# Second attention of a two-block transformer step: three weight splits cut into quarter pieces

## The chip, the cores and the metric

One core of a Trainium2 chip runs the whole program in one launch. The metric is the device time in microseconds (us); the median of several executions counts. Of an execution with the profiler on there is a trace, with the begin and end of each engine's instructions.

TensorE (PE in the rows) multiplies, ScalarE (ACT) and VectorE (DVE) work element by element, GpSimd (POOL) computes a few inverse roots, and SyncE (SP) issues nearly all loads.

## The reference, cut to what matters

256 tokens of width 1024, float32, batch 1. The first block is a modulated transformer layer: `h = rms_norm(x) * (1 + sc) + sh`, one projection `h @ w_in`, two attentions, gates, a projection `w_out` and a gated feed-forward part. The second block has four feed-forward parts, a short convolution and a compressed/selected/window attention. The change lies in the first block only:

```python
proj = h @ w_in[l]
(q_a, k_a, v_a, q_i, k_i, w_i, q_b, k_b, v_b, gate_a, gate_b) = jnp.split(proj, split_at, axis=-1)
o_a = dsa_attention(q_a, k_a, v_a, q_i, k_i, w_i)   # 4 heads of 128; each query keeps the 64 keys
                                                    # of highest index score
o_b = moba_attention(q_b, k_b, v_b)                 # 4 heads; with 256 tokens plain causal attention
merged = sigmoid(gate_a) * (o_a @ w_br_dsa[l]) + sigmoid(gate_b) * (o_b @ w_br_moba[l])
x = x + gt_m * (merged @ w_out[l])
```

## The kernel before, in words

**Products.** Float32 accuracy comes from three products of rounded halves: every operand is held as a high part (`fp32r`) and a low part, and `three` (L1713 to L1717) issues high times high, weight-low times high, weight-high times low. A weight unit is 128x2048 words (1 MB), four row blocks of 512 columns. A product of 1024 rows by 512 columns takes two units, each 24 matmuls of 512 columns.

**A unit's way.** SyncE loads it into one of three raw slots (`raw_ring`, L771). ScalarE rounds it into `w_hi_ring` (`split`, L910 to L917) when the raw slot is full and TensorE has used the unit three earlier. VectorE subtracts it into `w_lo_ring` (`lo_split`, L1244 to L1247), and by that tells TensorE that the unit is ready and SyncE that the raw slot is free (`raw_done`). SyncE goes through its list of loads in order, each waiting for the load three earlier to be freed. Modulation rows (`mod`, `mod_row`, `mod_sum`) use the same raw slots; TensorE reads them raw (L1853).

**The order of work** is one list, written by hand in `make_plan`. Each engine goes through the whole list and issues what is its own, so the list is the order of each engine's queue. `part(stage, chunk, number, parts, after, inside, held)` adds a unit: its matmuls, in four quarters where `inside` has four lists, with `inside[q]` behind quarter q; then the items of `after`; and then, unless `held`, `then split`, which splits all units up to the third one further.

**The units here**: V0 and V1 (`va`), then G0 to G3 (`gb`: chunk 0 parts 0 and 1, chunk 1 parts 0 and 1), B0, A0, B1, A1 (`bb`, `ba`) and `out1`. Before the change G1 is split behind V0, G2 behind V1, G3 behind G0, B0 behind G1, A0 behind G2.

**The second attention** (`dsa`) has eight items (four heads, two tiles of 128 queries) laid between the quarters of G0, G1 and G2 by `attention` and `spread`. Step i holds: `qk` i on TensorE (L1967, 128 wide for even items, 256 for odd ones); `sm` i on VectorE (L1547: mask, scale, maximum) and the exponential on ScalarE (L1128); transpose of the probabilities of item i-1 on TensorE (L1936), copied by ScalarE for even items (L1046) and by VectorE for odd ones (L1405); `pv` i-2 on TensorE (L1974), scaled by VectorE (L1551, L1554). The ten steps are spread over twelve quarters: G0 has none behind its first, then steps 0, 1, 2; G1 has 3, 4, none, 5; G2 has 6, 7, 8, 9. Behind G2 stand the transposes of `o` (L1882), which wait for the last scaled output.

**Top-k** (L1525 to L1537, VectorE) masks all but 64 keys of a query tile by rounds of `max` and `match_replace`, in four pieces per tile; the last one also writes `mask_d`, which the `sm` of this attention read.

Of the kernel before, what the change touches and what calls it, by code (L numbers as in the profile page):

```python
# [7 lines left out]
ALU = mybir.AluOpType  # L8
ACT = mybir.ActivationFunctionType
F32 = mybir.dt.float32  # L10
# [13 lines left out]
RING = 3  # L24
# [66 lines left out]
def make_plan():  # L91


    plan, units = [], []
# [14 lines left out]
    def tgroup(stage, n, **a):  # L109
        return [dict(a, kind="tp", stage=stage, g=g) for g in range(n)]  # L110
# [112 lines left out]
        if not last:  # L223
            add("then split", unit=u)

    def part(stage, chunk, number, parts, after=(), inside=(), held=False):


        subs = len(inside) if inside else 1
        for q in range(subs):  # L230
            add("lin", stage=stage, chunk=chunk, part=number, parts=parts, unit=len(units), sub=q, subs=subs)
            if inside:
                plan.extend(inside[q])
        units.append((stage, chunk, number))
        for a in after:
            plan.extend(a)
        if not held:
            add("then split", unit=len(units) - 1)
# [4 lines left out]
    def evac(stage, chunk=0):  # L243
        return [dict(kind="evac", stage=stage, chunk=chunk)]
# [4 lines left out]
    def mod(m, half):  # L249
        return [dict(kind="mod", m=m, half=half)]  # L250
# [4 lines left out]
    def mod_row(m, half):  # L255
        return [dict(kind="tp", stage="mrow", g=m, c=half)]
# [4 lines left out]
    def mod_sum(m):  # L261
        return [dict(kind="tp", stage="mod", g=m)]

    def topk(tt, piece):
        return [dict(kind="topk", tt=tt, piece=piece)]
# [34 lines left out]
    part("qa", 0, 1, 2, [mod_row(7, 1), evac("qa"), mod(8, 0)])  # L300
    part("ka", 0, 0, 2, [mod_sum(7), mod_row(8, 0), mod(8, 1), topk(1, 1)])
    part("ka", 0, 1, 2, [tgroup("qa", 2), mod_row(8, 1), evac("ka"), mod(9, 0)])
    part("va", 0, 0, 2, [mod_sum(8), mod_row(9, 0), mod(9, 1), topk(1, 2)])
    part("va", 0, 1, 2, [tgroup("ka", 2), mod_row(9, 1), evac("va"), topk(1, 3)])
    steps = attention([dict(b="dsa", h=h, tt=tt) for h in range(NH) for tt in range(TT)])
    inside = spread(steps, 3)
    part("gb", 0, 0, 2, [], inside[0])
    part("gb", 0, 1, 2, [evac("gb")], inside[1])
    part("gb", 1, 0, 2, [tgroup("o", 4)[:2]], inside[2])
    part("gb", 1, 1, 2, [evac("gb", 1), tgroup("o", 4)[2:]])  # L310
    add("sigmoid")
    part("bb", 0, 0, 1, [mod(10, 0)])
# [66 lines left out]
    for item in plan:  # L379
        if item["kind"] == "then split":  # L380
            split(item["unit"] + RING)
            continue
        full.append(item)
        if item["kind"] == "lin" and "sub" not in item:
            split(item["unit"] + RING)
        if item["kind"] == "gp":
            split(item["unit"] + RING)
        if item["kind"] == "ffn":
            n = 3 * NJ
            item["have"] = s  # L390
            s = min(item["unit"] + n + RING, len(units))
# [21 lines left out]
    for item in full:  # L413
        k = item["kind"]
        item["n"] = number("kind " + k)
        if k == "split":
            unit_raw[item["unit"]] = transfer("unit", item["unit"])
        if k == "mod":
            item["raw"] = transfer("mod", item["m"], item["half"])
        if k == "lin" and item["part"] == 0 and item.get("sub", 0) == 0:  # L420
            if (item["stage"], item["chunk"]) in (("cm", 0), ("qg", 0), ("wo", 0)) and count["pi"] % 2:
                number("pi")
            pi = THIRD if (item["stage"], item["chunk"]) == ("qg", 1) else number("pi")
            pi_of[item["stage"], item["chunk"]] = item["pi"] = pi
            item["pair_before"] = count.get(f"pair{pair_no(pi)}", 0)
        elif k in ("lin", "evac"):
            item["pi"] = pi_of[item["stage"], item["chunk"]]
        if k == "lin" and item.get("by_tt") and item["sub"] == 0:
            item["half"] = number("half")
        if k == "evac":  # L430
            st = item["stage"]
            if item.get("tt") == 0:
                item["half"] = count["half"] - 1
            if st not in ("out1", "co", "wo") and item.get("tt") != 0:
                pair_after[item["pi"]] = number(f"pair{pair_no(item['pi'])}") + 1
            if st in ("qi", "qb", "kb", "qa", "ka"):
                item["rope"] = number("rope")
            if st in ("qb", "kb", "qa", "ka", "qg") or (st == "kv" and item["chunk"]):
                item["nq"] = number("nq")
        if k == "cmp" and item["s"] == 0:  # L440
            item["nq"] = number("nq")
        if k == "tp":
            item["tg"] = number("tg")
            if item["stage"] == "mrow":
                item["of"] = number("mrow") // 2
            if item["stage"] in PAIRED:
                item["hl"] = number("hl")
            if item["stage"] != "p" and last_p is not None and item["tg"] - last_p[0] <= 2:
                item["outputs"] = last_p[1] + 1
            if item["stage"] == "p":  # L450
                last_p = item["tg"], count.get("it tp", 0)
        if k == "ffn":
            item["tg"], item["hl"], item["gi"] = number("tg", NJ), number("hl", NJ), number("gi", NJ)
            for u in range(item["have"], min(item["unit"] + 3 * NJ + RING, len(units))):
                unit_raw[u] = transfer("unit", u)
        if k == "xh":
            item["hl"] = number("hl")
        if k == "gp" and item["half"]:
            item["gi"] = number("gi")
        if k == "gt":  # L460
            item["tg"], item["gi"] = number("tg"), count["gi"] - 1
        if k in ("gu", "ffn", "nsa"):
            item["pairs_before"] = [count.get(f"pair{q}", 0) for q in range(2)]
        if k in ("qk", "sm", "pv") or (k == "tp" and item["stage"] == "p"):
            item["it"] = number("it " + k)
# [33 lines left out]
def turn(r):  # L499

    return (r - EARLY) // RING + 1
# [6 lines left out]
def two_block_program(nc, A, out):  # L508
# [40 lines left out]
    with ExitStack() as ctx:  # L549
# [5 lines left out]
        def sem(name):  # L555
            if name not in sems:
                sems[name] = ctx.enter_context(nc.semaphore(name))
            return sems[name]
# [339 lines left out]
        def _(act):  # L898
# [11 lines left out]
            def split(u, r, gate):  # L910

                act.wait_ge(sem(f"raw_full{r % RING}"), 32 * turn(r))
                if gate is not None:

                    act.wait_ge(sem("unit_used"), gate)
                words = unit_size(u)
                act.activation(w_hi[:, u % RING, 0:words], raw[:, r % RING, 0:words], ACT.Copy)\  # L917
                   .then_inc(sem("hi_ready"), 1)

            for item in plan:  # L920
# [5 lines left out]
                if k == "split":  # L926
                    u = item["unit"]
                    split(u, unit_raw[u], u - RING + 1 if u >= RING else None)
                if k == "square":
                    n = item["n"]  # L930
                    if n == 0:
                        act.wait_ge(sem("x_full"), 16)
                    else:
                        act.wait_ge(sem("x_ready"), 4 * xu[n])
                        act.wait_ge(sem("rstd_ready"), n)
                    if n == 6:
                        act.wait_ge(sem("qss_ready"), find["nq", "kv", 2] + 1)
                    for tt in range(TT):
                        ins = act.activation(junk[:, :], x[:, tt, :], ACT.Square, accum_out=ss[:, tt:tt + 1])
                        tick.step(ins) if tt < TT - 1 else ins.then_inc(sem("ss_ready"), 1)  # L940
# [298 lines left out]
        def _(dve):  # L1239
# [4 lines left out]
            def lo_split(u, r, two=lambda a: 0):  # L1244
                dve.wait_ge(sem("hi_ready"), u + 1 + two(3))
                words = unit_size(u)
                dve.tensor_tensor(w_lo[:, u % RING, 0:words], raw[:, r % RING, 0:words],  # L1247
                                  w_hi[:, u % RING, 0:words].bitcast(F32), ALU.subtract).then_inc(sem("raw_done"), 1)
# [74 lines left out]
            for item in plan:  # L1323
# [3 lines left out]
                    lo_split(u, unit_raw[u])  # L1327
                if k == "split":
                    lo_split(item["unit"], unit_raw[item["unit"]])
                if k == "init":  # L1330
                    dve.wait_ge(sem("init_done"), 1)
                    tick(dve.tensor_copy(cols1[:, :], bank[4][:, 0:P]))
                    dve.tensor_copy(cols2[:, :], bank[4][:, P:P + 56]).then_inc(sem("cols_ready"), 1)
                    dve.wait_ge(sem("cols_ready"), 1)
# [795 lines left out]
```

## Time and profile before

| | us |
|---|---|
| median of 3 runs | 1532.31 (1532.15 to 1532.56) |
| the profiled execution | 1530.0 |
| its span | 1528.0 |
| TensorE busy | 1465.4 (96%) |
| VectorE busy | 850.2 (56%) |
| ScalarE busy | 688.6 (45%) |
| GpSimd busy | 37.4 (2%) |
| second attention, first matmul of G0 to the transposes of `o` | 191.98 to 225.41 |

Durations of matmuls overlap, since the next one begins while the last drains: the time from one start to the next is what TensorE spends on one. Times of day in the text are us from the start of the span. The granted clock is that of TensorE, 1.00 for 2.4 GHz and 0.50 for 1.2 GHz.

### The profile page before, as it was taken

The numbers are of one execution on the slowest core, as the hardware profiler recorded it, in microseconds if no ns is written. First come the engines' busy times: TensorE is split into PE (matmuls) and PEld (weight loads), VectorE is DVE, ScalarE is ACT, GpSimd is POOL, SyncE is SP. The second block draws the span as 40 slices with busy tenths as digits, with TensorE's granted clock in tenths as the row PEclk, the third lists the DMA queues.
The fourth block names the chain that finished last, engine by engine and source line by source line (L and its number), as shares of the span: only waits on it lengthen the run. The fifth ranks groups of instructions, "written<-read, shape, count | busy, mean of one in ns | idle before, by whom it ended". The sixth has DMA issues, their size and how long they took to land.

```text
span 1528.0 us, 18024 instructions
## 1 busy us (share of the span) xinstructions
PE 1465.4 (96%) x6944; PEld 1169.2 (77%) x6944; DVE 850.2 (56%) x1023; ACT 688.6 (45%) x866; POOL 37.4 (2%) x53
## 2 busy tenths in 40 slices
PE   6989979999999999999999999989999988999998
PEld 3647667688888888888888888778888765788887
DVE  2676756554545554456764445566445567654453
ACT  2535444353334444444454444744444575554432
POOL 0010100000000000000000000210000020000000
PEclk9999999999999999999999999999999998999999
DMA  9853845555555566546555555555655430255552
GB/s 338 280 187 111 269 145 189 169 180 184 188 191 162 197 193 192 191 140 220 173 185 193 179 181 190 145 165 193 193 190 176 163 110 1 86 190 184 180 191 78
DMA packets 187881, 270.11 MB, mean 177 GB/s; under 512 B 8351, under 2 KB 134119, under 8 KB 187817
## 3 DMA queue, kind: packets, MB, share of 16 engines
q1 hardware_dynamic: 186448, 267.01, 53.5%
q10 hardware_dynamic: 1208, 1.94, 0.4%
q0 software_dynamic: 160, 0.26, 0.2%
q8 instruction: 44, 0.72, 0.2%
q14 instruction: 21, 0.16, 0.0%
HBM read 268.15 MB, written 1.05 MB: 176 GB/s over the span
## 4 chain that ended last, share of the span: by engine, by line
PE 84%; DVE 6%; ACT 4%; DMA 3%; issue 2%; POOL 0%; SPq 0%; ACTq 0%; DVEq 0%
PE bank L1715 25%; PE bank L1717 25%; PE bank L1716 25%; DVE w_lo_ring L1247 2%; ACT w_hi_ring L917 2%; PE bank L1745 2%; DMA raw_ring<-in_w_in_dram 1%; PE bank L1853 1%; PE bank L1882 1%; PE bank L2037 1%; PE bank L1940 1%; DMA raw_ring<-in_w_out_dram 1%; DMA arena<-in_w_mod_dram 1%; PE bank L2016 0%; DVE h_lo L1380 0%
## 5 line engine op out<-in xcount | busy, mean ns | idle before, releaser
L1247 DVE TENSOR_TENSOR w_lo_ring<-raw_ring,w_hi_ring 128x2048 fp32r<-128x2048 f32 x231 | 525.2, 2277 | 427.9 <-ACT w_hi_ring L1199 332.4
L1715 PE MATMUL bank<-w_hi_ring,h_hi 128*128 128x512 f32 x1360 | 544.1, 400 | 8.2 <-DVE h_lo L1380 3.1
L1717 PE MATMUL bank<-w_hi_ring,h_lo 128*128 128x512 f32 x1360 | 532.2, 391 | 0.0
L1716 PE MATMUL bank<-w_lo_ring,h_hi 128*128 128x512 f32 x1360 | 531.5, 391 | 0.0
L1199 ACT ACTIVATE w_hi_ring<-raw_ring 128x2048 fp32r<-128x2048 f32 x158 | 302.8, 1916 | 295.8 <-PE bank L1717 293.6
L1715 PEld LDWEIGHTS bank<-w_hi_ring,h_hi 128*128 128x128 f32 x1360 | 256.4, 189 | 77.1 <-issue 26.6
L1717 PEld LDWEIGHTS bank<-w_hi_ring,h_lo 128*128 128x128 f32 x1360 | 256.2, 188 | 55.3
L1716 PEld LDWEIGHTS bank<-w_lo_ring,h_hi 128*128 128x128 f32 x1360 | 256.8, 189 | 49.7
L1715 PE MATMUL bank<-w_hi_ring,f_hi 128*128 128x512 f32 (+1 forms) x456 | 177.4, 389 | 0.0
L1717 PE MATMUL bank<-w_hi_ring,f_lo 128*128 128x512 f32 (+1 forms) x456 | 176.5, 387 | 0.0
L1716 PE MATMUL bank<-w_lo_ring,f_hi 128*128 128x512 f32 (+1 forms) x456 | 176.2, 386 | 0.0
L917 ACT ACTIVATE w_hi_ring<-raw_ring 128x2048 fp32r<-128x2048 f32 (+1 forms) x73 | 136.7, 1880 | 85.3 <-PE bank L1717 40.3
L1207 ACT ACTIVATE glu_s<-bank,rstd 128x256 f32<-128x256 f32 x88 | 36.9, 471 | 142.0 <-PE bank L1717 142.0
L1715 PEld LDWEIGHTS bank<-w_hi_ring,f_hi 128*128 128x128 f32 (+1 forms) x456 | 85.0, 186 | 17.9 <-issue 1.1
L1717 PEld LDWEIGHTS bank<-w_hi_ring,f_lo 128*128 128x128 f32 (+1 forms) x456 | 85.0, 186 | 17.3
L1716 PEld LDWEIGHTS bank<-w_lo_ring,f_hi 128*128 128x128 f32 (+1 forms) x456 | 85.1, 187 | 16.8
L1665 DVE SCALAR_TENSOR_TENSOR glu_a<-bank,rstd,glu_s 128x256 f32<-128x256 f32 x88 | 38.5, 479 | 64.8 <-ACT glu_s L1207 64.8
L1671 DVE TENSOR_TENSOR f_lo<-bank,f_hi 128x512 fp32r<-128x512 f32 x55 | 37.6, 684 | 10.3 <-ACT f_hi L1213 10.3
L1213 ACT ACTIVATE f_hi<-bank 128x512 fp32r<-128x512 f32 x55 | 32.0, 582 | 20.9 <-PE bank L1745 20.9
L971 ACT ACTIVATE h_hi<-bank,cols 128x256 fp32r<-128x256 f32 x56 | 21.9, 475 | 33.2 <-PE bank L1882 33.2
L1153 ACT ACTIVATE arena<-bank,mn,arena 128x128 f32<-128x128 f32 (+1 forms) x64 | 31.9, 519 | 10.7 <-DVE mn L1570 10.6
L1745 PE MATMUL bank<-const,glu_a 128*128 128x128 f32 x236 | 35.3, 271 | 0.0
(252 smaller groups left out, 869.1 us busy)
## 6 DMA issues: line engine op xcount, KB each, us to landing
raw_ring<-in_ffn_w_gate_up_dram SPq DMA_DIRECT2D x176, 512.0 KB
raw_ring<-in_ffn_w_down_dram SPq DMA_DIRECT2D x44, 1024.0 KB
raw_ring<-in_w_in_dram SPq DMA_DIRECT2D x22, 1024.0 KB
raw_ring<-in_w_gate_up_dram SPq DMA_DIRECT2D x44, 512.0 KB
arena<-in_w_mod_dram SPq DMA_DIRECT2D x12, 1024.0 KB, 7.7
raw_ring<-in_w_mod_dram SPq DMA_DIRECT2D x12, 1024.0 KB
raw_ring<-in_w_down_dram SPq DMA_DIRECT2D x11, 1024.0 KB
raw_ring<-in_conv_w_in_dram SPq DMA_DIRECT2D x16, 512.0 KB
```

Of the source, the lines that this page charges most:

```text
L917: act.activation(w_hi[:, u % RING, 0:words], raw[:, r % RING, 0:words], ACT.Copy)\
L1153: ins = act.activation(p_n[:, step % 2, 2 * j + br, 0:n], bank[j][:, br * n:br * n + n], ACT.Exp, scale=rqp[:, qt, h:h + 1], bias=mn[:, c: ...
L1199: act.activation(w_hi[:, u % RING, :], raw[:, unit_raw[u] % RING, :], ACT.Copy)\
L1207: act.activation(glu_s[:, tt, :], glu_bank(f, jb, tt)[:, 0:GC], ACT.Silu, scale=rstd[:, tt:tt + 1] if f else 1.0).then_inc(sem("sg_ready"), 1)
L1213: act.activation(f_hi[:, jb % 2, :, :].rearrange("p a b -> p (a b)"), bank[6 + tg % 2][:, :], ACT.Copy).then_inc(sem("hi_t"), 1)
L1247: dve.tensor_tensor(w_lo[:, u % RING, 0:words], raw[:, r % RING, 0:words], w_hi[:, u % RING, 0:words].bitcast(F32), ALU.subtract).then_inc ...
L1665: dve.scalar_tensor_tensor(glu_a[:, tt, :], glu_bank(f, jb, tt)[:, GC:2 * GC], rstd[:, tt:tt + 1] if f else 1.0, glu_s[:, tt, :], ALU.mult ...
L1671: dve.tensor_tensor(f_lo[:, jb % 2, :, :].rearrange("p a b -> p (a b)"), bank[6 + tg % 2][:, :], f_hi[:, jb % 2, :, :].rearrange("p a b -> ...
L1715: pe.matmul(dst, hi, whi, start=start, stop=False)
L1716: pe.matmul(dst, hi, wlo, start=False, stop=False)
L1717: return pe.matmul(dst, lo, whi, start=False, stop=stop)
L1745: ins = pe.transpose(bank[6 + tg % 2][:, kk * T + tt * P:kk * T + (tt + 1) * P], glu_a[:, tt, kk * P:(kk + 1) * P], ident)
```

## The change

The splits of G2, G3 and B0 are taken out from behind V1, G0 and G1 (`held=True`). In their place `part(..., pieces=True)` adds `then piece` behind each quarter's `inside`: piece q of the unit three further than the one before this, so G2 inside G0, G3 inside G1, B0 inside G2. A piece is 512 of the 2048 columns: one `activation` copy on ScalarE and one subtraction on VectorE. The first piece on ScalarE has the waits of a whole split; the last on VectorE gives `raw_done`. The fourth piece of the second tile's top-k goes from behind V1 to behind V0. The order of the loads stays.

```diff
+            if pieces:
+                add("then piece", unit=len(units) - 1, q=q)
...
-    part("va", 0, 0, 2, [mod_sum(8), mod_row(9, 0), mod(9, 1), topk(1, 2)])
-    part("va", 0, 1, 2, [tgroup("ka", 2), mod_row(9, 1), evac("va"), topk(1, 3)])
+    part("va", 0, 0, 2, [mod_sum(8), mod_row(9, 0), mod(9, 1), topk(1, 2), topk(1, 3)])
+    part("va", 0, 1, 2, [tgroup("ka", 2), mod_row(9, 1), evac("va")], held=True)
...
-    part("gb", 0, 0, 2, [], inside[0])
-    part("gb", 0, 1, 2, [evac("gb")], inside[1])
-    part("gb", 1, 0, 2, [tgroup("o", 4)[:2]], inside[2])
+    part("gb", 0, 0, 2, [], inside[0], held=True, pieces=True)
+    part("gb", 0, 1, 2, [evac("gb")], inside[1], held=True, pieces=True)
+    part("gb", 1, 0, 2, [tgroup("o", 4)[:2]], inside[2], pieces=True)
...
+        if item["kind"] == "then piece":
+            u = item["unit"] + RING
+            if item["q"] == 0:
+                assert s == u
+                s += 1
+            full.append(dict(kind="piece", unit=u, q=item["q"]))
+            continue
...
-        if k == "split":
+        if k == "split" or (k == "piece" and item["q"] == 0):
...
+                if k == "piece":
+                    u, q = item["unit"], item["q"]
+                    r, cols = unit_raw[u], slice(512 * q, 512 * q + 512)
+                    if q == 0:
+                        act.wait_ge(sem(f"raw_full{r % RING}"), 32 * turn(r))
+                        act.wait_ge(sem("unit_used"), u - RING + 1)
+                    ins = act.activation(w_hi[:, u % RING, cols], raw[:, r % RING, cols], ACT.Copy)
+                    ins.then_inc(sem("hi_ready" if q == 3 else "hi_quarter"), 1)
...
+                if k == "piece":
+                    u, q = item["unit"], item["q"]
+                    r, cols = unit_raw[u], slice(512 * q, 512 * q + 512)
+                    if q < 3:
+                        dve.wait_ge(sem("hi_quarter"), 3 * (item["n"] // 4) + q + 1)
+                    else:
+                        dve.wait_ge(sem("hi_ready"), u + 1)
+                    ins = dve.tensor_tensor(w_lo[:, u % RING, cols], raw[:, r % RING, cols], w_hi[:, u % RING, cols].bitcast(F32), ALU.subtract)
+                    ins.then_inc(sem("raw_done"), 1) if q == 3 else tick(ins)
```

## Rows read from the trace of the kernel before

**Rows 1.** The page: busy time of TensorE, and the chain by engine.

```profile
PE 1465.4 (96%) x6944; PEld 1169.2 (77%) x6944; DVE 850.2 (56%) x1023; ACT 688.6 (45%) x866; POOL 37.4 (2%) x53
PE 84%; DVE 6%; ACT 4%; DMA 3%; issue 2%; POOL 0%; SPq 0%; ACTq 0%; DVEq 0%
```

**Rows 2.** Timeline of TensorE: start, us, line, operation [idle before, releaser].

```profile
191.98 0.50 PE L1715 MATMUL bank<-w_hi_ring,h_hi 128*128 128x512 f32 x1
...
195.01 0.47 PE L1715 MATMUL bank<-w_hi_ring,h_hi 128*128 128x512 f32 x1
...
196.48 0.59 PE L1967 MATMUL bank<-arena 128*128 128x256 f32 x2
199.30 0.30 PE L1936 MATMUL bank<-const,arena 128*128 128x128 f32 x1 [2.22 <-issue]
...
205.25 0.38 PE L1967 MATMUL bank<-arena 128*128 128x128 f32 x2
207.40 0.41 PE L1936 MATMUL bank<-const,arena 128*128 128x128 f32 x2 [1.76 <-ACT arena L1128]
...
215.05 0.59 PE L1967 MATMUL bank<-arena 128*128 128x256 f32 x2
218.85 0.30 PE L1936 MATMUL bank<-const,arena 128*128 128x128 f32 x1 [3.21 <-DVE arena L1554]
...
219.56 0.77 PE L1715 MATMUL bank<-w_hi_ring,h_hi 128*128 128x512 f32 x1
...
222.27 0.52 PE L1936 MATMUL bank<-const,arena 128*128 128x128 f32 x2
...
225.41 1.07 PE L1882 MATMUL bank<-const,arena 128*128 128x128 f32 x8 [0.56 <-issue]
...
243.67 1.07 PE L1853 MATMUL bank<-raw_ring,c_act 128*32 128x512 f32 x8
```

**Rows 3.** Windows: busy of PE, PEld, DVE, ACT, POOL; granted clock; DMA share; GB/s.

```profile
221.00:222.30 1.30, 1.30 (x5) 0.90 (x4) 0.00 (x0) 0.00 (x0) 0.00 (x0) 0.50 0.84 318
...
191.90:225.40 33.50, 25.75 (x128) 20.86 (x125) 18.64 (x49) 11.82 (x27) 0.00 (x0) 0.95 0.47 157
...
1208.00:1212.00 4.00, 4.00 (x15) 3.20 (x13) 2.02 (x7) 0.79 (x2) 0.72 (x2) 0.50 0.83 268
```

**Rows 4.** Timeline of VectorE around the low halves and the top-k.

```profile
193.36 0.42 DVE L1531 MAX8 top<-arena 128x8 f32<-128x256 f32 x1
...
196.11 2.29 DVE L1247 TENSOR_TENSOR w_lo_ring<-raw_ring,w_hi_ring 128x2048 fp32r<-128x2048 f32 x1
198.32 0.34 DVE L1547 CUSTOM_DVE_ANT_0 arena<-bank,arena,rq 128x128 f32<-128x128 f32 x1
...
203.97 2.29 DVE L1247 TENSOR_TENSOR w_lo_ring<-raw_ring,w_hi_ring 128x2048 fp32r<-128x2048 f32 x1 [1.57 <-ACT w_hi_ring L917]
206.18 0.48 DVE L1547 CUSTOM_DVE_ANT_0 arena<-bank,arena,rq 128x256 f32<-128x256 f32 x1
...
215.35 2.29 DVE L1247 TENSOR_TENSOR w_lo_ring<-raw_ring,w_hi_ring 128x2048 fp32r<-128x2048 f32 x1 [3.12 <-ACT w_hi_ring L917]
```

**Rows 5.** Timeline of ScalarE: a high half and an exponential.

```profile
202.04 1.90 ACT L917 ACTIVATE w_hi_ring<-raw_ring 128x2048 fp32r<-128x2048 f32 x1
206.70 0.51 ACT L1128 ACTIVATE arena<-arena,mn 128x256 f32<-128x256 f32 x1 [2.76 <-DVE mn L1547]
```

**Rows 6.** Groups by line and form, 160 to 260: busy, mean ns of one.

```profile
L985 ACT ACTIVATE h_hi<-bank 128x512 fp32r<-128x512 f32 x6 | 3.3, 601 | 12.7 <-PE bank L1882 12.7
...
L1263 DVE TENSOR_TENSOR arena<-glu_s,glu_a 128x512 f32<-128x512 f32 x4 | 2.8, 693 | 0.1
```

**Rows 7.** SyncE's issues of loads: start, us in the queue.

```profile
192.87 0.39 SPq L771 DMA_DIRECT2D raw_ring<-in_w_br_moba_dram  x1
198.43 0.39 SPq L771 DMA_DIRECT2D raw_ring<-in_w_br_dsa_dram  x1
```

**Rows 8.** Waits of TensorE from 225.5 to 312: total, times, longest.

```profile
PE bank L1715 <- issue: 1.8, 1, 1.8
```

More of the change, by code:

```diff
@@ L224, in by_token_tile, with part @@
             add("then split", unit=u)
-    def part(stage, chunk, number, parts, after=(), inside=(), held=False):
+    def part(stage, chunk, number, parts, after=(), inside=(), held=False, pieces=False):
         subs = len(inside) if inside else 1
```

## The prediction

> **What bounds the kernel now.** I read the page's first part and its chain of waits first: TensorE is busy 96% of the span and carries 84% of the chain [rows 1]. So a change to ScalarE or VectorE work is worth only what it takes out of TensorE's pauses. The changed stretch is the second attention, laid between the quarter units of gb. On TensorE's timeline it runs from the first matmul of gb's first unit (G0) at 191.98 to the transposes of o at 225.41, 33.43 us [rows 2]. In it TensorE pauses three times, always ahead of an L1936 transpose of probabilities: 196.91 to 199.30 (2.4 us), 205.48 to 207.40 (1.9) and 215.48 to 218.85 (3.4). (A pause is counted from where the qk matmuls ahead of it have issued: 0.43 us after the start of a 256-wide one, 0.22 after a 128-wide one. The idle column counts from their modelled end.) During the third the granted clock falls to 0.50 [rows 3], the 1.2 GHz level, and the work behind it issues at half pace: 6 weight matmuls take 2.71 us (219.56 to 222.27) where the six from 195.01 take 1.47, and with the small ones beside them this costs 1.6 us. A last pause of 0.6 us lies before 225.41. Pauses and slow clock make 9.9 us, leaving 23.6 us of matmul issue.
>
> The VectorE timeline tells where the pauses come from [rows 4]. Each is a whole split of 128x2048 in front of a short step: the low half of G2 from 196.11 sets the first sm (L1547) at 198.32, that of G3 from 203.97 sets sm at 206.18 though its logits were there by 203.5, and that of B0 from 215.35 sets the one at 217.56. Each of these low halves had itself waited for the high half on ScalarE (192.26, 202.04, 213.40; 1.9 us each) [rows 5]. The exponential starts 0.38 us after a 128-wide sm and 0.52 after a 256-wide one; the transpose follows the exponential by 0.60 or 0.70.
>
> **The change part by part.** The three splits stay the same words: G2 moves from behind V1 to G0's quarters, G3 from behind G0 to G1's, B0 from behind G1 to G2's. One high half and one low half become four each, 128x512. No row has exactly this form. For ScalarE, 128x512 takes 0.60 us [rows 6]; from start to start I take 0.55, since neighbours overlap a little (on VectorE the next one starts 0.08 before the end of a 2.29 one [rows 4]). The bounds are 0.48 (a quarter of the 1.90 of a whole split [rows 5], no fixed part) and 0.60 (no overlap). For VectorE a 128x512 operation takes 0.69, 0.60 from start to start [rows 6]; bounds 0.57 (a quarter of 2.29 [rows 4]) and 0.69. So a unit costs 2.2 instead of 1.8 us on ScalarE and 2.4 instead of 2.21 on VectorE. Three units add 1.2 and 0.6 us of work to engines that are busy 11.8 and 18.6 us of these 33.5 [rows 3]: hidden, as long as no step stands in the chain. So the pieces have no term of their own; they are followed in the schedule below.
>
> A rule of the Trainium skill speaks against cutting ("VectorE: DVE Perf Modes", the section on the TRN2 errata): every operation from SBUF pays a fixed extra time, an fp32 tensor_tensor lasting (N+151)/0.96 ns, 691 for 512 columns. The 0.69 row agrees; if nothing of it overlapped, each piece would stand 0.09 us longer before the next sm than I take, which the slack below mostly absorbs.
>
> Top-k: topk(1,3) is 193.36 to 196.11 on VectorE, 2.75 us [rows 4]. Moved behind topk(1,2), it starts at 189.25, fills 1.3 us in which VectorE waited for G1's high half, and ends at 192.0. The low half of G1 then runs 192.0 to 194.2 instead of 190.55 to 192.76. Nobody on TensorE waits: G1 is read from 199 on. SyncE does: B0's load, issued at 192.87 when G1's raw slot came free [rows 7], goes to about 194.3, and lands by 200 (a load takes 5 us); its first piece is wanted at 210.4.
>
> Now the schedule by the durations above. VectorE: mod-row sum to 194.8, low piece 0 to 195.4 (high piece 0 is done at 192.9), sm0 at 195.4. That is 2.9 earlier than 198.32, and is the sum: 2.21 of G2 gone, 1.3 of idle time used, 0.60 of the piece put in. Exponential at 195.8; transpose 0 possible at 196.4, TensorE arrives at 196.9: **the first pause goes, 2.4 us**. Then each step has the same ring: exponential, high piece (0.60+0.04), low piece (0.60), next sm. It gives sm1 at 197.45, transpose 1 possible at 198.7 just as TensorE arrives; sm2 at 199.95; transpose 2 is held until 201.2 by the scaling of output 0 (L1554) behind sm2, **a new pause of 0.25 us**. sm3 comes at 202.0, exponential 202.5, transpose 3 possible at 203.2, TensorE there at 203.4: **the second pause goes, 1.9 us**. G1's last quarters carry two pieces and one step: sm5 at 207.2, high piece 3 at 208.4, evacuation of gb (two operations of 0.60 with overlap, 1.0) to 210.0, so exp6 waits for ScalarE until 210.05, not for sm6 (209.65). Transpose 6 is possible at 210.9 and TensorE arrives at 211.4: **the third pause goes, 3.4 us, and with it the slow clock behind it, 1.6 us**. In G2: sm7 at 211.7, transpose 7 possible at 212.9, TensorE at 213.4. The tail is last: low piece 2 stands before the last scaling, which ends at 216.25; TensorE has issued pv7 at 215.6, so it waits 0.8 us instead of 0.6.
>
> Sum: 2.4 + 1.9 + 3.4 + 1.6 = 9.3 removed, 0.25 + 0.2 added: 8.8 us less; o begins at 216.6 instead of 225.41.
>
> Moved with the splits are three frees of the raw ring. SyncE's issue at 198.43 comes at about 202.0, and the two behind it, at 206.29 and 217.67 (of three alike rows the first stands), at 209.7 and 217 [rows 7]. The weights they bring (A0, B1, and the mod load) are wanted behind the o transposes at the earliest, 217 plus; landing at 207, 215 and 222 they are in time: the mod load is read at 243.67 now [rows 2], 235 then. Priced uncovered, each would be late by what it slipped, 3.6 us at most. Behind 225 every wait I find (1.8 us at 246.50 is the longest up to 300 [rows 8]) is on work that moves along with TensorE, so the gain should be kept.
>
> Against the profiled execution's 1530.0 us (span 1528.0 and 2.0 around it): 1521.2. The median of the three runs is 2.3 above it; carried to it, 1532.3 - 8.8 = **1523.5 us**.
>
> **The rivals.** *A, the ring runs late.* All eight steps share one ring ScalarE, VectorE, ScalarE: with a copy of probabilities in it 0.52 + 0.52 + 0.2 + 0.64 + 0.6 = 2.5 us for a wide step, 2.0 for a narrow one, against 2.2 us of TensorE work a step (six weight matmuls 1.47, attention 0.75). Nothing spare. If each handover is 0.15 us longer than I take, four handovers over eight steps bring back 8 x 0.6 = 4.8 us less the slack (0.5 each at transposes 0, 6 and 7): 3.3, gain 5.5, 1526.8. For it: the slack at transposes 1, 3 and 7 is 0 to 0.5 us. Against: the handovers are read from this stretch. 15%.
>
> *B, slower than before.* Low piece q stands on VectorE in front of the next sm, and waits for high piece q, queued on ScalarE behind an exponential. In the old order only three sm's had a split before them. If a piece's pair took 2.3 us or more instead of 1.24 (nearly a whole 2048 split's fixed part each time), the ring would be 3.4 us and the ten steps about 34 us: no gain, then 1.0 us lost for each 0.1 us further. At 2.6 us for the pair: 1535. That would need both 128x512 operations at twice their rows. 3%.
>
> *C, the slow clock comes elsewhere.* Granted 0.50 also shows at 1208 to 1212, behind pauses of the third attention [rows 3]; everything there begins 8.8 us earlier relative to whatever the chip samples. One such stretch more or less is worth 1.6 us, as the one here; two more would leave a gain of 5.6: 1526.7. The three runs of before lie within 0.41 us, which speaks against large swings. 7%, as much to the good side (1520.5). The Trainium skill ("TensorE: Matmul & The Clock Gate", Part 1) has it that the gate's sampling runs free and the number of slow matmuls changes from run to run; by that rule the result would scatter by such stretches, and the spread of 0.41 here does not show it.
>
> *D, nothing arrives.* The later loads or a chain at 244 to 300 that doesn't move take the gain back: 1530 to 1532. For it: DMA share is high there. Against: each issue there waits for a TensorE or VectorE event of its own stage. 5%.
>
> **How the numbers follow.** The forecast holds 70%, with its own range 1522.4 (all 9.9 us go) to 1525.5 (every piece at its upper bound, 0.14 us a step over eight steps, 1.1, and 0.9 of clock). A 15, C 7, D 5, B 3. Stretched by C below and A above, with B and D left out, it becomes 1521.5 to 1528. About 0.2%, 3.1 us, is what a measurement tells from no change: faster 0.92 (forecast, A, C), same 0.05, slower 0.03.
>
> **What would show it.** Right: sm0 at about 195.4; 128x512 forms of L917's and L1247's operations near 0.60 and 0.69 us, twelve each; no pause over 0.5 us before L1936; clock 1.00 from 192 to 217; o transposes at 216 to 217; the rest shifted by the same amount. Wrong: pauses of 0.5 us or more before most L1936 (A), VectorE waiting on ScalarE's pieces for more than 6 us in all (B), low clock in new windows (C), or a gap to the old trace that shrinks between 225 and 300 (D).

## The result and the profile after

The changed kernel takes 1521.2 us (median of 4, 1519.11 to 1522.11) against 1532.23 for the one before (median of 4); the ratio is 0.9931, 95% interval 0.9914 to 0.9948. Timed again later, it took 1522.05 (6 executions) against 1531.32 (11), ratio 0.9934 (0.9921 to 0.9948). So the gain was 11.0 us the first time and 9.3 the second. Over the 50 later executions of before and all 10 of the changed kernel the medians are 1531.4 and 1521.8, a difference of 9.6 us where 8.8 were forecast. The traced execution of the changed kernel has a span of 1519.8.

TensorE's timeline of the stretch, from the first matmul of G0 to the transposes of `o` (lines have moved: L1741 is the weight matmul, L1993 the qk, L1962 the transpose of probabilities, L2000 the pv, L1908 the transposes of `o`):

```profile
192.49 0.50 PE L1741 MATMUL bank<-w_hi_ring,h_hi 128*128 128x512 f32 x1
...
196.95 0.59 PE L1993 MATMUL bank<-arena 128*128 128x256 f32 x2
197.38 0.27 PE L1962 MATMUL bank<-const,arena 128*128 128x128 f32 x1
...
198.88 0.38 PE L1993 MATMUL bank<-arena 128*128 128x128 f32 x2
199.29 0.41 PE L1962 MATMUL bank<-const,arena 128*128 128x128 f32 x2
...
201.15 0.59 PE L1993 MATMUL bank<-arena 128*128 128x256 f32 x2
201.80 0.30 PE L1962 MATMUL bank<-const,arena 128*128 128x128 f32 x1
...
211.62 0.59 PE L1993 MATMUL bank<-arena 128*128 128x256 f32 x2
212.05 0.27 PE L1962 MATMUL bank<-const,arena 128*128 128x128 f32 x1
...
215.83 0.61 PE L2000 MATMUL bank<-arena 128*128 128x128 f32 x4
217.00 1.06 PE L1908 MATMUL bank<-const,arena 128*128 128x128 f32 x8 [0.56 <-issue]
```

Where rows 2 have pauses of 2.4, 1.9 and 3.4 us, the transpose now follows its qk matmuls after their own time (0.43 us for a 256-wide one, 0.22 for a 128-wide one). Two small pauses stand at transposes 1 and 2: 0.19 us (199.10 to 199.29) and 0.22 (201.58 to 201.80). The transposes of `o` start 1.17 us after the last pv, as in rows 2's trace, whose line for it is this:

```profile
224.24 0.61 PE L1974 MATMUL bank<-arena 128*128 128x128 f32 x4
```

The stretch lasts 24.51 us instead of 33.43, 8.9 less.

VectorE's timeline, first steps: pieces (L1354) in front of the sm steps (L1573):

```profile
192.62 2.29 DVE L1264 TENSOR_TENSOR w_lo_ring<-raw_ring,w_hi_ring 128x2048 fp32r<-128x2048 f32 x1
194.83 0.68 DVE L1389 TENSOR_TENSOR arena<-bank,arena 128x512 f32<-128x512 f32 x1
195.43 0.68 DVE L1354 TENSOR_TENSOR w_lo_ring<-raw_ring,w_hi_ring 128x512 fp32r<-128x512 f32 x1
196.03 0.34 DVE L1573 CUSTOM_DVE_ANT_0 arena<-bank,arena,rq 128x128 f32<-128x128 f32 x1
...
197.46 0.69 DVE L1354 TENSOR_TENSOR w_lo_ring<-raw_ring,w_hi_ring 128x512 fp32r<-128x512 f32 x1 [1.08 <-ACT w_hi_ring L944]
198.07 0.48 DVE L1573 CUSTOM_DVE_ANT_0 arena<-bank,arena,rq 128x256 f32<-128x256 f32 x1
```

The first sm starts 3.54 us after G0, where rows 4 have it at 6.34: 2.8 earlier. The two forms whose prices were taken from neighbours, in the groups of this stretch (busy us, mean ns of one, then idle us before them):

```profile
L1354 DVE TENSOR_TENSOR w_lo_ring<-raw_ring,w_hi_ring 128x512 fp32r<-128x512 f32 x12 | 8.2, 689 | 6.0 <-ACT w_hi_ring L944 6.0
L944 ACT ACTIVATE w_hi_ring<-raw_ring 128x512 fp32r<-128x512 f32 x12 | 7.1, 618 | 0.1
```

VectorE waited 6.0 us in all for ScalarE's pieces, just the line that the forecast had drawn as a sign of rival B. TensorE's pauses in the stretch show little of it.

Not all 8.9 us reach the next stage in this trace. TensorE's timeline ahead of B1 and the windows around it (columns as in rows 3):

```profile
238.07 0.62 PE L1741 MATMUL bank<-w_hi_ring,h_hi 128*128 128x512 f32 x1 [1.77 <-issue]
...
250.73 1.06 PE L1908 MATMUL bank<-const,arena 128*128 128x128 f32 x8 [0.34 <-DVE arena L1471]
```

```profile
192.50:217.00 24.50, 23.85 (x128) 19.74 (x125) 17.91 (x51) 12.77 (x35) 0.00 (x0) 1.00 0.53 173
236.00:238.00 2.00, 0.30 (x4) 0.00 (x0) 1.97 (x3) 0.60 (x1) 0.00 (x0) 1.00 0.05 7
238.00:241.50 3.50, 3.43 (x9) 2.68 (x10) 0.00 (x0) 0.00 (x0) 0.00 (x0) 0.53 1.00 379
```

The pause of 1.8 us before B1 is the one of before (rows 8), but now the granted clock behind it falls to the 1.2 GHz level (0.53 as the mean of 238.0 to 241.5), which costs 1.7 us. In the old trace there was none behind it. The clock in the attention is 1.00 throughout.

At one more place the slow clock went the other way. A pause of 3.1 us in the second block is in both kernels. The first matmul behind it and the window around its end, before and then changed (0.66 and 1.00 are the granted clocks):

```profile
997.48 0.77 PE L1715 MATMUL bank<-w_hi_ring,h_hi 128*128 128x512 f32 x1 [3.12 <-DVE h_lo L1380]
996.00:1001.00 5.00, 3.52 (x9) 2.83 (x10) 4.97 (x8) 2.50 (x3) 2.14 (x1) 0.66 1.04 354
```

```profile
990.76 0.47 PE L1741 MATMUL bank<-w_hi_ring,h_hi 128*128 128x512 f32 x1 [3.13 <-DVE h_lo L1406]
989.00:994.00 5.00, 3.24 (x16) 2.71 (x17) 5.00 (x8) 2.77 (x4) 1.86 (x1) 1.00 1.02 346
```

### The profile page after: what moved, and what is told of

It is laid out like the page before. It is cut to its first block, busy times and chain, and to the rows that moved or that the text cites. A ratio compares the mean times of both kernels' runs of the same rounds, so it can differ in the third digit from the quotient of the medians.

```text
span 1519.8 us, 18042 instructions
## 1 busy us (share of the span) xinstructions
PE 1465.2 (96%) x6944; PEld 1168.5 (77%) x6944; DVE 851.5 (56%) x1032; ACT 689.8 (45%) x875; POOL 37.4 (2%) x53
## 4 chain that ended last, share of the span: by engine, by line
PE 85%; DVE 6%; ACT 4%; DMA 2%; issue 2%; SPq 1%; POOL 0%; ACTq 0%; DVEq 0%
PE bank L1741 25%; PE bank L1743 25%; PE bank L1742 25%; DVE w_lo_ring L1264 2%; PE bank L1771 2%; ACT w_hi_ring L926 2%; PE bank L1879 1%; DMA arena<-in_w_mod_dram 1%; PE bank L1908 1%; PE bank L2063 1%; PE bank L1966 1%; DMA raw_ring<-in_w_in_dram 1%; SPq L830 0%; PE bank L2042 0%; DVE h_lo L1406 0%
## 5 line engine op out<-in xcount | busy, mean ns | idle before, releaser
L1264 DVE TENSOR_TENSOR w_lo_ring<-raw_ring,w_hi_ring 128x2048 fp32r<-128x2048 f32 (+1 forms) x228 | 518.4, 2277 | 420.3 <-ACT w_hi_ring L1216 332.4
L1741 PE MATMUL bank<-w_hi_ring,h_hi 128*128 128x512 f32 x1360 | 544.6, 400 | 6.1 <-DVE h_lo L1406 3.1
L1741 PEld LDWEIGHTS bank<-w_hi_ring,h_hi 128*128 128x128 f32 x1360 | 256.6, 189 | 75.8 <-issue 24.6
L1741 PE MATMUL bank<-w_hi_ring,f_hi 128*128 128x512 f32 (+1 forms) x456 | 177.4, 389 | 0.0
L926 ACT ACTIVATE w_hi_ring<-raw_ring 128x2048 fp32r<-128x2048 f32 (+2 forms) x70 | 131.1, 1879 | 84.4 <-PE bank L1743 41.5
L1741 PEld LDWEIGHTS bank<-w_hi_ring,f_hi 128*128 128x128 f32 (+1 forms) x456 | 85.0, 186 | 17.9 <-issue 1.1
```

The source lines that it names most:

```text
L1741: pe.matmul(dst, hi, whi, start=start, stop=False)
```

## The experiments

Three figures are used to compare: the time from the first matmul of G0 to the transposes of `o`; "slow clock", the busy time of TensorE times (1 - granted clock), summed over windows of 1 us; and medians. All but c1 were timed against before; its medians in those comparisons lie between 1531.3 and 1531.7.

| kernel | G0 to `o`, us | slow clock in it | median, us (executions) | ratio to before, 95% |
|---|---|---|---|---|
| before, first and second trace | 33.43, 33.43 | 1.7, 1.6 | 1531.4 (50) | |
| changed, first and second trace | 24.51, 24.40 | 0, 0 | 1521.8 (10) | 0.9931 and 0.9934 |
| e1 top-k only | 30.44 | 0 | 1526.5 (7) | 0.9974 (0.9962, 0.9987) |
| e2 pieces only | 25.72 | 0 | 1522.8 (5) | 0.9949 (0.9936, 0.9962) |
| e3 whole, moved | 30.36 | 1.6 | 1526.5 (8) | 0.9968 (0.9955, 0.9981) |
| e4 halves | 25.45 | 0 | 1522.4 (5) | 0.9944 (0.9931, 0.9957) |
| e5 high half whole | 24.68 | 0 | 1521.2 (6) | 0.9935 (0.9921, 0.9949) |
| e6 A1 later | 24.33 | 0 | 1521.3 (6) | 0.9934 (0.9921, 0.9947) |
| e7 shifted | 24.38 | 0 | 1528.3 (12) | 0.9974 (0.9963, 0.9985) |
| e8 A1 and O0 later | 24.36 | 0 | 1519.4 (6) | 0.9920 (0.9903, 0.9937) |
| e9 low pieces twice | 31.99 | 0 | 1527.9 (12) | 0.9981 (0.9971, 0.9991) |

One execution of e3 took 2950 us and is left out.

**e1, the top-k piece alone.**

```diff
-    part("va", 0, 0, 2, [mod_sum(8), mod_row(9, 0), mod(9, 1), topk(1, 2)])
-    part("va", 0, 1, 2, [tgroup("ka", 2), mod_row(9, 1), evac("va"), topk(1, 3)])
+    part("va", 0, 0, 2, [mod_sum(8), mod_row(9, 0), mod(9, 1), topk(1, 2), topk(1, 3)])
+    part("va", 0, 1, 2, [tgroup("ka", 2), mod_row(9, 1), evac("va")])
```

> Top-k piece moved, the three splits whole and where they were before. My theory (the pauses come from 2.2 us low halves standing before the sm steps; the top-k move only fills 1.3 us in which VectorE waited): the low half of G2 starts 1.3 us earlier, so the first pause shrinks from 2.4 to about 1.1 us, the pauses of 1.9 and 3.4 us stay; o transposes about 1.3 us earlier after the first matmul of G0 than before (32.1 instead of 33.4 us), time 1.3 us below before. Rival (the top-k piece was the main cause of the first pause and with it of the rest): all pauses shrink, 4 us or more.

TensorE's rows with a pause, between G0 and `o`:

```profile
198.84 0.30 PE L1936 MATMUL bank<-const,arena 128*128 128x128 f32 x1 [0.89 <-issue]
206.93 0.41 PE L1936 MATMUL bank<-const,arena 128*128 128x128 f32 x2 [1.76 <-ACT arena L1128]
218.39 0.30 PE L1936 MATMUL bank<-const,arena 128*128 128x128 f32 x1 [3.22 <-DVE arena L1554]
```

The first pause shrank by 1.3 us (2.22 to 0.89 in the idle column) and the other two stayed to 0.01 us, as my theory had it. The stretch is 3.0 us shorter, not 1.3: behind the same pause of 3.2 us this trace shows no slow clock, and that is the other 1.6. The median is 4.9 us below before, which the schedule does not explain; the mean clock of its executions is 0.9887 against 0.9863. That excess of 3.6 us stays open.

**e2, the pieces alone** (`topk(1, 3)` back behind V1, the rest as changed).

```diff
-    part("va", 0, 0, 2, [mod_sum(8), mod_row(9, 0), mod(9, 1), topk(1, 2), topk(1, 3)])
-    part("va", 0, 1, 2, [tgroup("ka", 2), mod_row(9, 1), evac("va")], held=True)
+    part("va", 0, 0, 2, [mod_sum(8), mod_row(9, 0), mod(9, 1), topk(1, 2)])
+    part("va", 0, 1, 2, [tgroup("ka", 2), mod_row(9, 1), evac("va"), topk(1, 3)], held=True)
```

> Pieces as in the change, top-k piece back behind V1. My theory: sm0 starts at 4.7 us after the first matmul of G0 instead of 3.5, transpose 0 is held about 0.8 to 1.0 us, the other pauses stay away; 24.5 + 0.9 = 25.4 us from G0 to the o transposes; gain over before about 8 us of stretch, so some 1 us less than the change. Rival (top-k carries much of the gain): the gain falls by 3 us or more.

```profile
198.44 0.30 PE L1962 MATMUL bank<-const,arena 128*128 128x128 f32 x1 [0.62 <-issue]
200.72 0.41 PE L1962 MATMUL bank<-const,arena 128*128 128x128 f32 x2 [0.39 <-issue]
```

25.72 us where 25.4 was expected: 1.2 more than with the top-k moved, in two pauses at transposes 0 and 1 (0.62 and 0.39 us in the idle column). The pieces, cut and moved together, carry 6.0 of the 7.2 us of schedule (the stretch without its slow clock), the top-k 1.2.

**e3, the splits moved but whole.**

```diff
-            if pieces:
-                add("then piece", unit=len(units) - 1, q=q)
+            if pieces and q == 2:
+                add("then split", unit=len(units) - 1)
```

> Splits not cut: G2, G3, B0 whole, each behind the third quarter of the unit in which the change has its four pieces; top-k moved as in the change. If cutting is what counts (my theory): each whole low half again stands before an sm or a scaling; pauses of about 2.4 us at transpose 2, 0.5 at transpose 5 and 2.9 before the o transposes; G0 to o about 28.5 to 29 us, that is 4.5 to 5 us of the 8.9 gained. If moving alone explains it (rival): within 1 us of the change, 24.5 to 25.5 us. Whether a slow clock follows a pause of over 2 us can't be told: 0 to 1.7 us more.

```profile
204.75 0.42 PE L1962 MATMUL bank<-const,arena 128*128 128x128 f32 x1 [2.68 <-DVE arena L1580]
214.89 0.41 PE L1962 MATMUL bank<-const,arena 128*128 128x128 f32 x2 [0.40 <-ACT arena L1145]
223.35 1.06 PE L1908 MATMUL bank<-const,arena 128*128 128x128 f32 x8 [1.81 <-issue]
```

The pauses are at the three places named, 2.7, 0.4 and 1.8 us, with a slow clock of 1.6 us behind the first. Without it the stretch is 28.8. Of the 7.2 us of schedule moving brings 2.9, and 1.3 of these are the top-k's; cutting brings the other 4.3. Pieces left in the old places were not run.

**e4, halves.**

```diff
+            if pieces and q % 2:
...
-                    r, cols = unit_raw[u], slice(512 * q, 512 * q + 512)
+                    r, cols = unit_raw[u], slice(1024 * (q // 2), 1024 * (q // 2) + 1024)
```

> Two pieces of 1024 columns a unit, behind the second and the fourth quarter, instead of four of 512. My theory (what stands before an sm is one piece pair of the ring, here about 1.05 + 1.15 us instead of 0.6 + 0.6): the steps behind a piece run 1.0 us later than in the change, half of them are covered by the slack of 0 to 0.5 us; pauses of 0.5 to 1 us at about four transposes: 26 to 27.5 us from G0 to o, gain over before 6 to 7.5 us of stretch. Rival (any cut will do, pieces of 512 bring nothing beyond halves): 24.5 us as in the change.

```profile
200.50 0.41 PE L1962 MATMUL bank<-const,arena 128*128 128x128 f32 x2 [0.73 <-issue]
213.48 0.30 PE L1962 MATMUL bank<-const,arena 128*128 128x128 f32 x1 [0.32 <-DVE arena L1580]
```

25.45 us, between the two theories and below my 26: two pauses in the idle column, 0.73 at transpose 1 and 0.32 at transpose 6. Nearly all of the gain is there with two pieces; the second cut is worth about 1.0 us in the traces, less than the medians can tell apart (1522.4 against 1521.8).

**e5, the high half whole.**

```diff
-                    ins = act.activation(w_hi[:, u % RING, cols], raw[:, r % RING, cols], ACT.Copy)
-                    ins.then_inc(sem("hi_ready" if q == 3 else "hi_quarter"), 1)
+                        act.activation(w_hi[:, u % RING, :], raw[:, r % RING, :], ACT.Copy).then_inc(sem("hi_ready"), 1)
```

> The change, but the high half of each unit whole (128x2048 on ScalarE, where the change has its first piece) and only the low half in four pieces. My theory (the ring scaling, exponential, high piece, low piece, next sm sets the pace): with the high halves of G3 and B0 ScalarE is held 1.3 us longer in one step of G1 and one of G2; the low piece and sm behind it come 1.2 us later once each, later pieces wait for nothing, so every other step is 0.6 us shorter; pauses of 0.5 us or less at two transposes: G0 to o 24.5 to 25.3 us, time within 1 us of the change. Rival (ScalarE's share of the cut is what removed the pauses): pauses of 1.5 us or more at transposes 4 and 7, 27 us or more.

```profile
215.03 0.41 PE L1959 MATMUL bank<-const,arena 128*128 128x128 f32 x2 [0.38 <-ACT arena L1144]
```

24.68 us, one pause of 0.38 at a late transpose. ScalarE need not be cut: the stretch is within 0.3 us of the changed kernel's and the median within 0.6. My reading is that what it loses in one step it wins in the next three, where the low piece waits for nothing. This is the simplest form with nearly the whole gain.

**e9, each low piece computed twice**, to double the suspected cost.

```diff
-                    ins = dve.tensor_tensor(w_lo[:, u % RING, cols], raw[:, r % RING, cols], w_hi[:, u % RING, cols].bitcast(F32), ALU.subtract)
+                    for again in range(2):
+                        ins = dve.tensor_tensor(w_lo[:, u % RING, cols], raw[:, r % RING, cols], w_hi[:, u % RING, cols].bitcast(F32), ALU.subtract)
+                        if again == 0:
+                            tick.step(ins)
```

> The change with each low piece computed twice on VectorE (the second time with the same operands), which takes 0.68 us more in every step. It measures the slack of the ring. My schedule left at transposes 0 to 7 slacks of 0.5, 0, (pause), 0.2, 1, 1, 0.5 and 0.5 us: 0.68 more in each of about ten steps, less the slack, gives pauses at most transposes from the second on, 3 to 5 us in all: G0 to o 27.5 to 29.5 us. Rival (the ring has much slack and TensorE alone sets the pace): under 25.5 us.

```profile
201.99 1.42 DVE L1355 TENSOR_TENSOR w_lo_ring<-raw_ring,w_hi_ring 128x512 fp32r<-128x512 f32 x2 [1.35 <-ACT w_hi_ring L944]
203.32 0.35 DVE L1576 CUSTOM_DVE_ANT_0 arena<-bank,arena,rq 128x128 f32<-128x128 f32 x1
```

```profile
201.37 0.41 PE L1965 MATMUL bank<-const,arena 128*128 128x128 f32 x2 [1.10 <-issue]
204.61 0.30 PE L1965 MATMUL bank<-const,arena 128*128 128x128 f32 x1 [0.79 <-DVE arena L1583]
...
214.58 0.41 PE L1965 MATMUL bank<-const,arena 128*128 128x128 f32 x2 [1.29 <-ACT arena L1145]
```

Each step grew by 0.73 us (1.42 against 0.69), and eleven pieces stand ahead of the last scaling: 8.0 us. The stretch grew by 7.5. So the slack over the whole stretch is about 0.5 us; I had expected it to cover about three or more. Both theories missed. The change just fits.

**c1 and c2, both kernels again.**

> The kernel before once more, for a second trace. My theory (the pauses and the schedule are the same in each execution, and where a slow clock follows one changes from one execution to the next): the same three pauses of 2.2, 1.8 and 3.2 us (idle column), G0 to o 31.7 us plus 0 or 1.6 to 1.7 us of slow clock; after the first matmul of G0 the span less the time lost to the slow clock is 1323 within 1.5 us. Rival (the slow clock behind the 3.2 us pause belongs to the pause): 33.4 us again with the slow clock in the same place, as a pause of 3.2 us in the kernel with the top-k move alone did not show.

> The changed kernel once more, for a second trace and more times. My theory: G0 to o 24.5 us again without a pause over 0.3 us before the tail; the slow clock that stood behind the 1.8 us pause of bb in its first trace is there or not by chance; median 1521 to 1522.5, that is 9 to 10 us below before: 7.2 of pauses and about 2 of slow clock that before has more often. Rival (the slow clock only moved behind the change to bb, for good): slow clock behind the bb pause again and a gain of no more than 8 us.

The stretches repeat: 33.43 again, to the hundredth, and 24.40. For before, the slow clock stands behind the 3.2 us pause again; in the changed kernel it stands behind the pause ahead of B1 again. In both the place is the one that the rivals named; e1 has the first pause without it, and e2 to e5 have the second without it. Elsewhere the slow clock does move between two traces of one kernel. Windows of before's first trace and of c1:

```profile
28.00:32.00 4.00, 4.00 (x24) 3.27 (x28) 1.57 (x4) 0.00 (x0) 0.00 (x0) 1.00 0.90 252
1270.00:1277.00 7.00, 5.95 (x22) 3.59 (x23) 6.57 (x18) 2.71 (x10) 0.00 (x0) 0.53 0.01 2
```

```profile
28.00:32.00 4.00, 4.00 (x11) 3.14 (x12) 1.44 (x3) 0.00 (x0) 0.00 (x0) 0.57 0.96 248
1270.00:1277.00 7.00, 5.34 (x34) 3.46 (x32) 6.51 (x20) 3.16 (x12) 0.00 (x0) 1.00 0.01 2
```

On c1 my figure for the rest missed: the span after G0's start less slow clock is 1325.1 where the first trace has 1323.3 and I had allowed 1.5 around 1323, so the slow-clock sum does not add up exactly to what it costs (presumably because part of it lies under waits).

**e7, everything from G0 on shifted.**

```diff
-    part("va", 0, 1, 2, [tgroup("ka", 2), mod_row(9, 1), evac("va")], held=True)
+    part("va", 0, 1, 2, [tgroup("ka", 2), mod_row(9, 1), hold(15, 4), evac("va")], held=True)
```

> The change with 15 idle matmuls (128x256) more on TensorE in front of G0, so that all from G0 on comes about 1.6 us later and the pause of 1.8 us ahead of B1 lies elsewhere in time by as much. In both traces of the changed kernel a slow clock of 1.7 us stood behind that pause, in none of the other kernels that have the same pause. My theory (where the slow clock falls depends on when a pause comes, not on which pause it is): no slow clock there in this trace, or in another place, and the median within 2 us of the change (1.6 us more work). Rival (the slow clock behind that pause belongs to the changed order): slow clock there again, median 1.6 us above the change.

The shift came out at 6.4 us (194.33 to G0's first matmul at 200.72), four times what I had put down: the trace has 30 matmuls for the 15 float32 ones, each of over 0.2 us. TensorE's rows:

```profile
194.33 6.74 PE L1802 MATMUL bank<-const 128*128 128x256 f32 x30
...
246.21 0.47 PE L1741 MATMUL bank<-w_hi_ring,h_hi 128*128 128x512 f32 x1 [1.77 <-issue]
```

The 4 us behind that pause, in c2 and in e7:

```profile
239.00:243.00 4.00, 3.85 (x10) 3.05 (x11) 0.05 (x1) 0.54 (x1) 0.00 (x0) 0.57 0.97 374
```

```profile
246.00:250.00 4.00, 3.79 (x17) 3.17 (x18) 0.10 (x1) 0.22 (x1) 0.00 (x0) 1.00 0.95 367
```

The same pause of 1.77 us, with a clock of 0.57 and 10 matmuls behind it in the one, 1.00 and 17 in the other. The median is 6.5 above the changed kernel, outside the 2 us of my expectation, and as much as the added work. e5, with the same order of work and the same pause, shows no slow clock either. So it doesn't belong to the changed order for good.

**e6 and e8, the pause ahead of B1.** e6 takes A1's split from behind B0 to behind the evacuation that B1 waits for; e8 also takes O0's split behind the evacuation of bb's second chunk:

```diff
-    part("bb", 0, 0, 1, [mod(10, 0)])
-    part("ba", 0, 0, 1, [evac("bb", 0), mod_row(10, 0), mod(10, 1)])
-    part("bb", 1, 0, 1, [mod_sum(9), mod_row(10, 1), hold(7, 4), evac("ba", 0), evac("bb", 1), tgroup("merged", 4)[:2]])
+    part("bb", 0, 0, 1, [mod(10, 0)], held=True)
+    part("ba", 0, 0, 1, [evac("bb", 0), [dict(kind="then split", unit=len(units) - 1)], mod_row(10, 0), mod(10, 1)], held=True)
+    part("bb", 1, 0, 1, [mod_sum(9), mod_row(10, 1), hold(7, 4), evac("ba", 0), evac("bb", 1), [dict(kind="then split", unit=len(units) - 1)], tgroup("merged", 4)[:2]])
```

> The change, and the split of A1 moved from behind B0 to behind the evacuation of bb's first chunk. In the change TensorE pauses 1.8 us ahead of B1 because that evacuation (1.3 us) stands on VectorE behind A1's low half, which waits for a high half behind the sigmoids. My theory: the pause goes or falls under 0.3 us, and with it the chance of a slow clock behind it (1.7 us in the one trace): 1.8 to 2.5 us less than the change. Rival (A1's own weights, or the modulation row behind it, become late): a new pause of 1 us or more before by-token A1 or before L1891, gain under 1 us.

> As the kernel with A1's split moved, and the split of O0 (w_out's first unit) also moved, from behind A0 to behind the evacuation of bb's second chunk. With A1 alone the 1.8 us pause only changed its place: 2.3 us before the transposes of merged, because the evacuation of ba stood on VectorE behind O0's low half (243.85 to 246.1), which waited for a load. My theory: the evacuation starts when the modulation sum is there, about 244.8, merged's transposes at about 54.4 us after G0 instead of 56.5 (slow clock taken off): 2.0 us less than the change, in the median 1.5 to 2.5. Rival (O0 is late instead): a new pause ahead of out1's first unit of 1 us or more, and no gain.

The transposes of merged in e6, then in e8:

```profile
249.60 1.06 PE L1908 MATMUL bank<-const,arena 128*128 128x128 f32 x8 [2.26 <-DVE arena L1471]
```

```profile
248.60 1.06 PE L1908 MATMUL bank<-const,arena 128*128 128x128 f32 x8 [0.34 <-DVE arena L1471]
```

In e6 the pause ahead of B1 is gone and stands again, 2.26 us long, ahead of merged: 56.59 us from G0 there, against 58.24 in the changed kernel, of which 1.7 are slow clock. Nothing is gained, and neither theory had named this place. In e8 it is gone for good: 54.71 us, close to the 54.4 expected. e8's median of 1519.4 is the lowest of all; its interval overlaps that of the changed kernel, so that it beats it rests on the 1.8 us in the trace. It is clear of before.

## Why the prediction was right

*The total.* The median of the first comparison, 1521.2, lies below the forecast's own range (1522.4 to 1525.5) and 0.3 us below the stretched one (1521.5 to 1528); the median of all ten, 1521.8, lies in the stretched one. The gain, 11.0, 9.3 and 9.6 us, was forecast as 8.8. What the change does to the attention was right nearly to the step; that the total fits as well is partly luck, as the slow clock below shows.

*First pause, 2.4 us: right.* It is gone. sm0 comes 2.8 us earlier instead of 2.9. The top-k carries 1.3 us of it (e1) and the pieces the rest. One reading behind it was wrong, without effect on the sum: the low half of G2 had not waited for its high half as the other two had (rows 4 show no idle time ahead of 196.11), it stood behind the top-k.

*Second and third pause, 1.9 and 3.4 us: right*, with the mechanism named, low halves in front of the sm steps: e1 keeps them to 0.01 us and e3 moves them to where the whole splits then stand.

*Added pauses, 0.45 us: measured 0.41*, but not where they were put. The one at transpose 2, forecast 0.25, measured 0.22. The 0.2 for a longer tail did not come: `o` starts 1.17 us after the last pv in both traces, and the idle column has 0.56 in both. In its place stands a pause of 0.19 at transpose 1, where the forecast had TensorE arrive just in time. So the stretch adds up: 7.7 us of pauses and 1.6 of slow clock gone, 0.4 added, 8.9. Piece prices, 0.60 and 0.69 us: measured 0.618 and 0.689.

*Slow clock, 1.6 us: the weak term.* The forecast took it with the pause as if bound to it. In the traces it followed the 3.2 us pause in two of three (both of before, not e1), the 2.7 us pause of e3 in one of one, a pause of 2.2 or 2.3 us in none of three, and the 1.8 us pause ahead of B1 in two of eleven, both the changed kernel's, where it takes the 1.6 back. Behind the 3.1 us pause of the second block it stands in ten of thirteen, both of before among them and neither of the changed kernel. From G0 to merged the first traces differ by 65.55 - 58.24 = 7.3 us, just the pauses. The Trainium skill ("TensorE: Matmul & The Clock Gate", Part 1) has the gate's sampling run free of the program, with slow matmuls varying between runs of one kernel. Those varying places agree with it, and so do the windows at 28 and 1270 us, where c1 differs from before's first trace. That the slow clock stood in the same place twice in each kernel does not speak against it: two traces of a kernel are too few to tell a fixed place from chance.

*Rival C was then half true.* The slow clock did come elsewhere, yet the median did not suffer: medians fell by 9.6, 2.3 more than the pauses. The executions show a mean granted clock of 0.9882 against 0.9863. Taken at the same clock the kernels are closer: at 0.987 the means are 1522.1 (6) and 1531.0 (4), at 0.990 they are 1519.9 (4) and 1527.1 (2), 8.9 and 7.2 apart. The rest of the gain thus goes with a slow clock that before has more often. No trace shows where: both traced executions of before have a clock above its mean (0.989 and 0.992). Why it has more stays open. So the 1.6 us of the sum came in with the right size from a source that the forecast had not named.

*Rival A did not happen, but its premise held.* I gave the ring 1.5 us of slack; e9 measures 0.5. The forecast was right because the handovers, read from the old trace, held (0.39 us from sm0 to its exponential, 0.52 from sm1 to its own, where 0.38 and 0.52 were taken) and the sm steps came within about 0.1 us of the schedule, not because there was room.

*Rivals B and D are out*: the piece pair costs 1.3 us, so the 6.0 us that VectorE waited for ScalarE lay in its spare time, and TensorE's waits behind 217 are those of before, 1.77 and 0.34.

## What to carry to other kernels

A long operation on a helper engine that has ample time on average can still stop the main one: look at what stands in its queue just ahead of each short step of a dependent chain, cut it to the size of a step and lay the pieces between the steps. Two pieces gave most of the gain here, and only the engine ahead of the short step needed the cut. When a pause goes, follow the queue behind it: the one ahead of B1 left only when two splits were moved, not one. And count a slow clock behind a pause as a chance, not as part of the pause: it takes more than a trace or two to know how often it comes.

## What the runs showed of the hardware

The pauses of the attention and the one ahead of B1 repeat between two traces of a kernel to 0.02 us, while whole times of one kernel spread over 8 us (before: 1526.7 to 1534.8 in 50 executions) along with the mean granted clock. The first three times of before, within 0.41 us, had suggested a much smaller spread. An episode of slow clock costs, by the measure of the table, most often 1.7 us, the shortest 1.4 (c1, at 998 us) and the longest 6.8 (e7, at 1251). A float32 matmul of 128x256 shows as two matmuls in the trace, 0.43 us in all (6.4 us for 15, e7).
